# One hybrid decoder trunk: the second layer's modulation weights loaded into the activations' buffer as one home of 512 columns instead of two homes of 256

## The reference, cut to what matters

```
cond = jax.nn.silu(c)
for l in range(DEPTH):
    mod = cond @ w_ada[l] + b_ada[l]
    sh_m, sc_m, g_m, sh_f, sc_f, g_f = jnp.split(mod, 6, axis=-1)
    h = rms_norm(x, norm_gain[l, 0]) * (1.0 + sc_m) + sh_m
    # layer 0: RWKV-7 heads and gated linear attention heads; layer 1: HGRN2 and SSD
    x = x + g_m * (head outputs @ w_out[l])
    # then a mixture of 16 experts, two for each token, with sh_f, sc_f, g_f
```

## Time and profile before

| | |
|---|---|
| median of 3 runs | 1513.36 us (1512.42 to 1519.51) |
| the profiled execution | 1519.4 us |
| its span, first to last instruction | 1517.6 us |
| TensorE busy | 1332.1 us (88%) |
| VectorE busy | 622.8 us (41%) |
| ScalarE busy | 299.0 us (20%) |
| mean DMA rate | 219 GB/s |
| mean granted share of TensorE's clock | 0.939 |

### The profile page before, as it was taken

One profiled execution on the slowest core, in us unless ns is written; L12 is line 12 of the kernel. 1 busy time (PEld: TensorE's weight loads), 2 busy tenths in 40 slices (PEclk: granted clock), 3 DMA queues, 4 the chain that ended last, 5 costly groups with the idle time before them and its releaser, 6 DMA issues.

```text
span 1517.6 us, 23238 instructions
## 1 busy us (share of the span) xinstructions
PE 1332.1 (88%) x10229; PEld 656.5 (43%) x10229; DVE 622.8 (41%) x953; ACT 299.0 (20%) x476; POOL 76.0 (5%) x231
## 2 busy tenths in 40 slices
PE   5999999588797797899999859998998789999992
PEld 3444444267665345333333344554453453333331
DVE  1134541465654226423323245476723553323334
ACT  3111211332231003000000042432212400000002
POOL 7100000000000000000000020000000000000002
PEclk9999999798989797999999989999999889999997
DMA  9773310442354008899999671111100699999994
GB/s 353 251 277 111 112 56 0 180 155 72 114 168 169 0 6 360 339 425 393 381 425 420 270 250 56 56 56 57 56 0 0 267 360 395 416 356 425 419 380 180
DMA packets 83632, 332.68 MB, mean 219 GB/s; under 512 B 6440, under 2 KB 29260, under 8 KB 66124
## 3 DMA queue, kind: packets, MB, share of 16 engines
q1 hardware_dynamic: 70176, 290.04, 49.1%
q10 hardware_dynamic: 7884, 21.24, 3.6%
q0 software_dynamic: 5472, 19.93, 3.4%
HBM read 308.65 MB, written 22.54 MB: 218 GB/s over the span
## 4 chain that ended last, share of the span: by engine, by line
PE 68%; DVE 14%; DMA 10%; ACT 5%; issue 2%; POOL 0%; SPq 0%; DVEq 0%; ACTq 0%; POOLq 0%
PE banks L1908 15%; PE banks L1415 15%; PE banks L1929 9%; DVE work L2044 6%; PE banks L1824 6%; PE banks L1404 3%; DMA h_features<-in_w_up_dram 3%; DMA h_features<-in_w_down_dram 2%; PE banks L1808 2%; DMA work<-h_rows,idx_tok 2%; PE banks L1337 2%; DVE work L2050 1%; DMA ring<-in_w_ada_dram 1%; PE banks L1887 1%; PE banks L1463 1%
## 5 line engine op out<-in xcount | busy, mean ns | idle before, releaser
L1415 PE MATMUL banks<-h_features,ring 128*128 128x512 f32 x640 | 284.7, 600 | 5.6 <-ACT h_features L1003 4.1
L1908 PE MATMUL banks<-ring,work 128*64 128x512 f32 (+1 forms) x672 | 202.8, 601 | 3.3 <-issue 2.3
L1908 PE MATMUL banks<-work 128*64 128x512 f32 (+1 forms) x672 | 199.7, 595 | 0.1
L1415 PEld LDWEIGHTS banks<-h_features,ring 128*128 128x128 f32 x640 | 120.5, 192 | 152.0 <-issue 147.4
L2044 DVE TENSOR_TENSOR work<-work,banks 128x256 f32<-128x256 f32 (+2 forms) x82 | 44.8, 569 | 172.7 <-PE banks L1908 132.0
L1908 PEld LDWEIGHTS banks<-ring,work 128*64 128x64 f32 (+1 forms) x672 | 60.5, 129 | 103.7 <-issue 99.0
L1929 PE MATMUL banks<-ring,work 128*64 128x512 f32 (+1 forms) x288 | 98.7, 593 | 2.3 <-DMA h_features<-in_w_down_dram 1.7
L1824 PE MATMUL banks<-y_features,ring 128*128 128x512 f32 x192 | 85.9, 610 | 6.4 <-DVE small L2576 6.4
L2044 DVE TENSOR_TENSOR work<-work 128x512 f32<-128x512 f32 (+8 forms) x168 | 86.1, 513 | 12.5 <-ACT work L1195 3.6
L1908 PEld LDWEIGHTS banks<-work 128*64 128x64 f32 (+1 forms) x672 | 60.0, 130 | 69.1 <-issue 65.7
L888 POOL DMA_INDIRECT work<-h_rows,idx_tok x20 | 19.1, 953 | 1217.7 <-DVE idx_tok L2712 895.8
(11 more groups left out here) (374 smaller groups left out, 1733.5 us busy)
## 6 DMA issues: line engine op xcount, KB each, us to landing
ring<-in_w_up_dram SPq DMA_DIRECT2D x16, 2048.0 KB, 15.0
work<-in_w_gate_dram SPq DMA_DIRECT2D x16, 2048.0 KB, 13.8
work<-in_w_up_dram SPq DMA_DIRECT2D x14, 2048.0 KB, 14.1
ring<-in_w_down_dram SPq DMA_DIRECT2D x12, 2048.0 KB, 13.7
ring<-in_w_ada_dram SPq DMA_DIRECT2D x11, 2048.0 KB, 9.5
h_features<-in_w_ada_dram SPq DMA_DIRECT2D x16, 1024.0 KB, 6.8
work<-in_w_down_dram SPq DMA_DIRECT2D x8, 2048.0 KB, 13.6
h_features<-in_w_down_dram SPq DMA_DIRECT2D x8, 2048.0 KB, 14.2
```

The source lines that it names most:

```text
L1415: ins = mm(PS[0:w, b, :], lhsT=W[:, k, c0:c0 + w], rhs=h[:, k, :], start=(k == 0), stop=(k == KD - 1))
L1908: ins = mm(PS[rows, bank, :], lhsT=xt[:, k, rows], rhs=w[:, k, :], start=(k == 0), stop=(k == KD - 1))
```

## The change

In `h_` the two homes of 256 columns become one of 512. Units 0 and 1 of a tile come in one load of 2 MB, and so do units 4 and 5. `half_place` for these gives the left or right 256 columns of each 512. The load for units 4 and 5 waits until unit 1 is done, and the load for units 0 and 1 of a later tile waits until unit 5 of the tile before is done, since either overwrites the whole buffer. Both count on `half_loaded0`. The number of bytes, the matmuls and the order of work on TensorE, VectorE, ScalarE and GpSimd stay as they were. SP issues 8 loads to `h_` instead of 16.

```diff
         def half_place(i):
 
-            home = y_ if i < GATE_HALVES else h_
-            return home[:, 2048 * (i % 2):2048 * (i % 2 + 1)].rearrange("p (k n) -> p k n", n=256)
+            if i >= GATE_HALVES:
+                return h_[:, :].rearrange("p (k n) -> p k n", n=512)[:, :, 256 * (i % 2):256 * (i % 2 + 1)]
+            return y_[:, 2048 * (i % 2):2048 * (i % 2 + 1)].rearrange("p (k n) -> p k n", n=256)
...
             def load_half(i):
                 t, m = tile_part(i)
-                if i in (GATE_HALVES, GATE_HALVES + 1):
+                if i == GATE_HALVES:
                     sp.wait_ge(sem("proj_done"), NB[0])
                 elif i > GATE_HALVES:
-                    sp.wait_ge(sem("unit_summed"), unit_done(*(tile_half(t, m - 4) if m >= 4 else tile_half(t - 1, m + 4))))
+                    sp.wait_ge(sem("unit_summed"), unit_done(*(tile_half(t, 1) if m == 4 else tile_half(t - 1, 5))))
                 else:
                     sp.wait_ge(sem("unit_summed"), unit_done("half", i - 2) if i >= 2 else unit_done("first", 0))
                 l, c = half_layer(i)
+                if i >= GATE_HALVES:
+                    sp.dma_start(h_[:, :].rearrange("p (k n) -> p k n", n=512),
+                                 A["w_ada"][l].rearrange("(k p) n -> p k n", p=P)[:, :, c:c + 512])\
+                      .then_inc(sem("half_loaded0"), 16)
+                    return
...
-                            for m in (0, 1, 4, 5):
+                            for m in (0, 4):
                                 load_half(tile_half(t, m)[1])
...
-                        before = (3, 2)[m % 2] + 2 * t + m // 4
-                        pe.wait_ge(sem(f"half_loaded{m % 2}"), 16 * (before + 1))
+                        pe.wait_ge(sem("half_loaded0"), 16 * (3 + 2 * t + m // 4 + 1))
```

## The result

The changed kernel took 1522.95 us (median of 15 runs, 1517.06 to 1526.08); the kernel before, in 15 runs on the same chips, 1513.39 us (1510.09 to 1521.06). The ratio is 1.0053 with a 95% interval of 1.0038 to 1.0067: 8.0 us slower, between 5.7 and 10.1. I had forecast 12.4 us and 1526 us. The 8.0 us lie just above the 7.6 us that I had called measurable, so the direction is clear, but not by much.

A forecast was written before the change was run, and what follows sets the result against it. It took TensorE to bound the kernel (68% of the span ends on it, 10% on DMAs). Waits 11.4 + clock 3 - gaps 2 = 12.4 us on 1513.36 us gave 1526 us, range 1517 to 1535.

The forecast's parts named there:

- The place and the cause: Before unit 4 in each tile, TensorE waits for the full 2 MB: 2.75, 2.59, 2.75 and 4.37 us late.
- My reason for 9.0 us: Loads to `h_`: 8.0 us with no instruction packet, 9.1 and 9.5 with one; two packets in tile 0, so 9.0.
- What is passed on: Unit 4's lateness reaches the end, less VectorE's slack in tile 0 and tile 3's old wait: 11.4 us.
- The clock, first side: Behind the new waits, TensorE's clock may fall to half, likeliest in tile 3: +3 us, between 0 and 8.
- my heavy rival: The clock falls in every tile, 2 us more per stall, with 9.5 us loads: 21.4 us, 1535 us; chance 0.15.
- Gaps at the end of solve: TensorE's gaps of 1.24, 0.74 and 1.83 us in `solve` may partly go: -2 us, between 0 and -3.8.
- The quick load: The load before unit 4 lands in about 6.8 us, costing 2.6 us: 1516 us; chance 0.13.
- the stretch behind gives it back: Gaps in `solve` return all 3.8 us, with 8.0 us loads and the clock unmoved: 3.6 us, 1517 us; chance 0.08.

The follow-up runs named there:

- issue alone: The kernel before with its two 1 MB loads for units 4 and 5 both waiting for unit 1, each unit waiting only for its own load: 1517.65 us, ratio 1.0012.
- both needed: The kernel before with both 1 MB loads for units 4 and 5 waiting for unit 1, and unit 4 waiting for both loads: 1519.99 us, ratio 1.0034.
- the longer wait: The changed kernel with the load for units 4 and 5 held back until unit 2 instead of unit 1: 1533.22 us, ratio 1.0109.

## Why the prediction was right, and where its sizes were off

**The place and the cause.** Right. Unit 4 waits for one load of 2 MB in each tile, the loads land 8.2, 9.2, 9.0 and 8.8 us after their issue (DMA view of each issue; I had taken 9.0 for all), and the waits are 1.85, 2.94, 2.64 and 4.15 us, where I had 2.75, 2.59, 2.75 and 4.37: 11.6 us against 12.5. That the wait comes from both units' weights having to be there before unit 4 is shown by the two runs with late loads: issue alone 1.0012 and 4.6 us of waits, both needed 1.0034 and 14.4 us. That units 0 and 1 matter little is shown, within 2 or 3 us, by the run that joins only units 4 and 5. The formula of the Trainium skill ("DMA: Bandwidth & Descriptors", "Anatomy of one DMA"), with its estimate of 6.8 us for 2 MB, was given for another path and is not borne out here by these four landings.

My reason for 9.0 us does not hold, though the number was near. I had set 8.0 us with no instruction packet against 9.1 and 9.5 us with one. But the view of the earlier trace rows ends at 386.9 us, 1 us before that load lands, and the DMA view of 386.9 to 387.8 us has a packet:

```profile
q8 instruction: 1, 0.02, 7.7%
```

Another ring load of the same trace, issued at 329.87 us, took 8.2 us with a packet in its time; and in the changed kernel the load of tile 0 took 8.2 us, also with one, and that of tile 3 took 8.8 us with two. So the packets do not sort the landings, and that the mean came to 8.8 us is in part luck.

**What is passed on.** I had taken 11.4 us. Beyond the first part it is about one for one (the longer wait). The inversions grew by 16.3 us, that is by the waits, less the 0.56 us that unit 5 had waited, plus about 5 us, which lie between the starts of units 4 and 5 (about 1.3 us more in each tile).

**The clock, first side.** I had +3 us, between 0 and 8. About 5 us in the inversions is inside, and in all four tiles the clock fell behind the wait: unit 5 took 1.30 us in tile 0 and 1.31 in tile 1, unit 4 took 1.28 in tile 2, and both took 1.93 in tile 3. This was the mechanism of my heavy rival, at its place, but not its total.

**The term that was mis-sized** is "Gaps at the end of solve", of which I took -2 us between 0 and -3.8. What came back behind the inversions was 10 to 13 us in the profiles. I had seen the gaps, and I had seen that the loads run while TensorE is late, but had priced only the gaps themselves. Gaps of TensorE without a releaser sum to 7.9, 4.8 and 9.3 us in the three profiles of before (318 to 515 us) and to 3.3 us in the changed kernel, so they make about 4 us of it, the far end of my term; the rest is the clock, which I had priced only on the side of the loss. In the kernel before `solve` of tiles 1 and 2 has half a clock in it or behind it each time, at 35.8 to 38.3 us for the stretch where 31 to 32 are possible; the changed kernel no longer has that in tile 1, but still in tile 2. Put together in the profiles: 16.3 - 13.2 = 3.1 us for 320 to 510 us, against a ratio of 8.0 us in the runs. The profiles of before differ by 7 us among themselves (spans of 1511.7, 1517.6 and 1518.9 us), so one profile of the changed kernel and three of before do not close the sum. What is measured as a total is the 8.0 us of 15 runs each. That it came out 4.4 us under the forecast is two errors of opposite sign: a larger loss in the inversions and a much larger return behind them.

**What stays open** is why a late unit 4 keeps the clock up in the `solve` behind it. Weights that move in `solve` have a part, since holding them back gains 7.3 us before. Yet the run with only a late issue had a stretch of 32.28 us after tile 1 with old loads there and a wait of only 0.93 us at unit 5, so a long wait is not what it takes. Where the idle pieces fall in time may matter, and I did not separate that from the gaps. Nor did I separate the shape of the load (two of 1 MB that must both be there, 1.0034; one of 2 MB, 1.0064 on the same chip).

**The rivals.** The quick load was wrong by its landings (8.2 us and more). That the stretch behind gives it back was right in kind and came with a larger size than its 3.8 us, but did not outweigh the wait. The heavy clock was right in that the clock fell in every tile, by about 1.3 us each and not 2, and only for the inversions.

## What to carry to other kernels

Two loads into two homes are not one load in two parts: each home is freed, filled and waited for by itself, and joining them moves the fill to the later release and the use to the later landing. Count the time between the last read of the joined home and its first new use, and set it against the landing time of the whole: here 4.7 to 6.5 us against 8.2 to 9.2. And price a stall on TensorE over the whole stage: here the clock added about 5 us behind the waits, and the stretches behind were some 10 us shorter, where the old schedule had lost the clock. When a transfer time is read from a view, let the view reach to the landing.

## What the runs showed of the hardware that I had not expected

- Extra matmuls of 3.3 us in each wait (5.4 us in tile 3) made the changed kernel 5.6 us faster, although unit 4 started 0.5 to 0.9 us behind the landing of its load in each tile; the granted clock then stayed at 2.4 GHz from 328 to 496 us.
- With q1 at 109.6% for 5 us no instruction packet moved, and TensorE stood still for 4.24 us without a releaser. It went on 2.2 to 2.7 us after the next packet. That is no rule for a full DMA, since elsewhere a packet moved with q1 at 103.8%, and a gap of 1.24 us stood where no weights moved.
- The kernel before with its prefetches held back until `solve` is nearly done is 0.5% faster (0.9952, 0.9928 to 0.9975), though the loads have less time: the earliest moment was not the best one.
